# Two layers' first norm: the sums are turned before they are scaled, and 1/rms is put on eight units at eviction

## What is computed

```python
x = x + peer_ffn(h2, ...)                 # end of the first block
x = rmsnorm(x, g_final)                   # x / sqrt(mean(x*x) + 1e-6) * g_final
for l in range(2):                        # the two layers
    h = rms_norm(x, norm1_g[l])
    z = h @ w_in[l]                       # 9 projections of 512 and the 4096 gate columns
    za, zb, zc, zd, zg = split(z)         # retention, conv, gmlp, window attention, gates
    a, gate = split(zb)                   # conv branch
    u = a * sigmoid(gate)                 # then a 31-tap depthwise convolution, layer norm, silu
    x = x + (mix of the four branches) @ w_out[l]
    h = rms_norm(x, norm2_g[l])
    x = x + (silu(gt) * up) @ w_ffn_out[l]
```

## Time and profile before

| | us |
|---|---|
| median of 3 runs | 2181.37 (2179.74 to 2186.02) |
| the profiled execution's own time | 2182.02 |
| its span in the trace | 2180.3 |
| TensorE busy in the span | 2145.6 (98%) |
| VectorE, ScalarE, GpSimd busy | 1345.5, 1230.4, 970.7 |
| mean granted TensorE clock | 0.997 of full speed |
| DMA: bytes and mean rate | 370.16 MB, 170 GB/s |

### The profile page before, as it was taken

How to read it: one execution, slowest core, us unless ns; L and a number is a source line. 1 busy time by engine, 2 the same in 40 slices (tenths; PEclk the granted TensorE clock), 3 DMA queues, 4 the chain that set the end, 5 groups by cost and what they waited for, 6 DMA issues and landing times.

```text
span 2180.3 us, 38720 instructions
## 1 busy us (share of the span) xinstructions
PE 2145.6 (98%) x15148; PEld 2013.9 (92%) x15148; DVE 1345.5 (62%) x2626; ACT 1230.4 (56%) x2201; POOL 970.7 (45%) x791
## 2 busy tenths in 40 slices
PE   8999999999999999999999999999999999999999
PEld 7898989999999998888888899999998999899997
DVE  3547652998666766666665765356664854546664
ACT  5667554456777765555555556645445465655443
POOL 4675546999666650000004785560001876561000
PEclk9999999999999999999999999999999999999999
DMA  6544455656444456666665554455665545455665
GB/s 210 155 144 126 155 184 171 187 181 187 145 139 144 144 172 204 193 194 193 194 193 169 181 164 144 129 178 171 185 200 164 181 145 160 132 164 170 187 193 157
DMA packets 102952, 370.16 MB, mean 170 GB/s; under 512 B 11370, under 2 KB 12787, under 8 KB 102133
## 3 DMA queue, kind: packets, MB, share of 16 engines
q1 hardware_dynamic: 102772, 367.69, 54.4%
HBM read 365.53 MB, written 2.11 MB: 169 GB/s over the span
## 4 chain that ended last, share of the span: by engine, by line
PE 87%; DVE 6%; ACT 4%; issue 1%; POOL 1%; DMA 1%; SPq 0%; DVEq 0%; ACTq 0%; POOLq 0%
PE stream_bank L557 16%; PE stream_bank L559 16%; PE stream_bank L558 16%; PE side_bank L557 11%; PE side_bank L558 11%; PE side_bank L559 10%; PE side_bank L846 1%; PE side_bank L845 1%; ACT unit_hi L1114 1%; PE side_bank L635 1%; DVE swa_var L2277 1%; POOL unit_lo L2414 1%; PE side_bank L682 1%; DVE unit_lo L1658 1%; PE side_bank L662 1%
## 5 line engine op out<-in xcount | busy, mean ns | idle before, releaser
L2414 POOL TENSOR_TENSOR unit_lo<-raw,unit_hi 128x512 fp32r<-128x512 f32 (+1 forms) x724 | 932.3, 1314 | 403.3 <-ACT unit_hi L1114 401.8
L1114 ACT ACTIVATE unit_hi<-raw 128x1024 fp32r<-128x1024 f32 (+1 forms) x678 | 708.5, 1045 | 197.5 <-PE side_bank L559 74.6
L1658 DVE TENSOR_TENSOR unit_lo<-raw,unit_hi 128x1024 fp32r<-128x1024 f32 (+1 forms) x316 | 390.2, 1235 | 225.5 <-ACT unit_hi L1114 225.1
L557 PE MATMUL stream_bank<-hT_hi,unit_hi 128*128 128x256 f32 x1360 | 402.1, 296 | 3.1 <-POOL unit_lo L2414 3.1
L559 PE MATMUL stream_bank<-hT_hi,unit_lo 128*128 128x256 f32 x1360 | 387.3, 285 | 0.0
L558 PE MATMUL stream_bank<-hT_lo,unit_hi 128*128 128x256 f32 x1360 | 387.1, 285 | 0.0
L557 PE MATMUL stream_bank<-h2T_hi,unit_hi 128*128 128x256 f32 x1152 | 329.6, 286 | 0.0
L559 PE MATMUL stream_bank<-h2T_hi,unit_lo 128*128 128x256 f32 x1152 | 326.0, 283 | 0.0
L558 PE MATMUL stream_bank<-h2T_lo,unit_hi 128*128 128x256 f32 x1152 | 325.8, 283 | 0.0
L557 PEld LDWEIGHTS stream_bank<-hT_hi,unit_hi 128*128 128x128 f32 x1360 | 262.8, 193 | 10.5 <-issue 4.6
L558 PEld LDWEIGHTS stream_bank<-hT_lo,unit_hi 128*128 128x128 f32 x1360 | 263.0, 193 | 1.5
(11 more groups left out here) (355 smaller groups left out, 4526.3 us busy)
## 6 DMA issues: line engine op xcount, KB each, us to landing
raw<-in_peer_u_dram SPq DMA_DIRECT2D x128, 512.0 KB, 3.6
raw<-in_peer_v_dram SPq DMA_DIRECT2D x128, 512.0 KB, 3.6
raw<-in_gate_dram SPq DMA_DIRECT2D x64, 512.0 KB, 3.6
raw<-in_gt_dram SPq DMA_DIRECT2D x44, 512.0 KB, 4.2
raw<-in_up_dram SPq DMA_DIRECT2D x44, 512.0 KB, 4.2
raw<-in_ffn_out_dram SPq DMA_DIRECT2D x44, 512.0 KB, 4.2
raw<-in_branch_dram SPq DMA_DIRECT2D x32, 512.0 KB, 3.7
raw<-in_w_gate_dram SPq DMA_DIRECT2D x24, 512.0 KB, 3.6
```

Source lines behind the costliest of these rows:

```text
L557: mm(out, l.hi, r.hi, start=start, stop=False)
L1114: activation(k.unit_hi[n % SPLIT_SLOTS][:, 0:w], k.raw[n % RAW_SLOTS][:, 0:w], ACT.Copy).then_inc(k.sem("unit_hi"), 1)
L1658: V.tensor_tensor(k.unit_lo[s][:, 0:w], k.raw[n % RAW_SLOTS][:, 0:w], k.unit_hi[s][:, 0:w], ALU.subtract).then_inc(unit_lo, 1)
L2414: last = G.tensor_tensor(k.unit_lo[s][:, cols], k.raw[n % RAW_SLOTS][:, cols], k.unit_hi[s][:, cols], ALU.subtract)
```

## The change

- The sums of X are turned as they are, with the identity, as soon as VectorE has added them (`added_turns` with `norm_turns(..., scaled=False)`); the gain goes on when the turned rows are split. For layer 0 the gain is g_final times norm1. The pair goes to `turned_sums` (in `ys`), not to `hT2`. The three `keep_warm` are gone.
- cg and ca are multiplied from this unscaled pair, and VectorE puts 1/rms on each of the eight units: cg by one product out of the bank (ScalarE's tanh then follows in place), ca by one product within the bank ahead of L2310. 1/rms comes as rows, by `token_rows` (two matmuls with ones, behind cg.1) and a copy.
- The scaled pair for all the later units is built in rounds 1 to 6: in rounds 1 to 4 VectorE writes two chunks each of `scaled` out of the banks, in rounds 4 and 5 ScalarE writes the high parts, in rounds 5 and 6 VectorE the low parts (two 128x512 subtractions in each). rqk.0 waits for them.
- Layer 0: both norms are worked out at once. VectorE multiplies X by g_final (`x_gained`, four pieces), ScalarE sums the squares of both. The final norm's output is written to X piece by piece in rounds 2 to 5 (`final`), the fourth ahead of the low parts in round 5.
- SyncE loads three units more before the constants' fetch, which still waits for the fourth `x_final`. GpSimd's masking moves from the layer's start to the round of gv.3. The bias table moves from round 6 to round 11.

The diff, cut to its core:

```diff
@@ pe_program
-        keep_warm("nl")
 
     def layer(l):
-        keep_warm(name("n1"))
-        for _ in norm_turns(k.X, name("n1")):
+        sums = "peer_v" if l == 0 else f"ffn_out.{l - 1}"
+        for _ in added_turns(lambda h, t: (sums, t, h), name("n1")):
             pass
         def bias_tables():
-            for _ in range(5):
+            for _ in range(10):
...
             for i in range(KM):
-                fm_unit(name("cg"), i, k.hT2, KD, ready=chunks_of(name("n1")) if i == 0 else None)
+                fm_unit(name("cg"), i, k.turned_sums, KD,
+                        ready=(lambda c: (k.sem("turned_lo"), KD // 2 * l + c // 2 + 1)) if i == 0 else None)
+                if i == 1:
+                    token_rows(name("n1"))
+                yield
+            for i in range(KM):
+                fm_unit(name("ca"), i, k.turned_sums, KD)
+                yield
+            for i in range(8):
+                fm_unit(name("rqk"), i, k.hT2, KD,
+                        ready=(lambda c: (k.sem("scaled_lo"), KD // 2 * l + c // 2 + 1)) if i == 0 else None)
@@ act_program, layer
-        norm_stats(name("n1"), k.X, ready, k.squares4)
-        for _ in norm_hi(name("n1"), name("norm1"), k.hT2):
+        turned = norm_hi(name("n1"), "final" if l == 0 else name("norm1"), k.turned_sums)
+        activation(k.small("root_t", 1), k.ones[:, 0:1], ACT.Sqrt)
+        next(turned)
+        for t in range(TILES):
+            for h in range(2):
+                act.wait_ge(*k.over[sums, t, h])
+            last = activation(junk[:, t, :], k.X[:, t, :], ACT.Square, accum_out=sq[:, t:t + 1])
+            next(turned)
+        for _ in turned:
             pass
+        def statistics():
+            done = last
+            if l == 0:
+                for t in range(TILES):
+                    act.wait_ge(k.sem("x_gained"), 2 * t + 2)
+                    done = activation(k.xg[:, t, :], k.xg[:, t, :], ACT.Square,
+                                      accum_out=sq[:, TILES + t:TILES + t + 1])
+            done.then_inc(k.sem("norm_squares"), 1)
+            roots = r if l == 0 else r[:, 0:TILES]
+            act.wait_ge(k.sem("norm_sums"), STATS[name("n1")])
+            activation(roots, roots, ACT.Sqrt, scale=1.0 / D).then_inc(k.sem("norm_roots"), 1)
+            yield
+            yield
+            yield
+            for k2 in range(KD // 2):
+                act.wait_ge(*k.over[name("n1"), k2])
+                pair = slice(2 * k2, 2 * k2 + 2)
+                split_hi(k.hT2.hi[:, pair, :], k.scaled[:, pair, :], "scaled_hi")
+                if k2 == 1:
+                    yield
+            yield
@@ dve_program, layer
+        def gained(t, cols):
+            V.tensor_tensor(k.xg[:, t, cols], k.X[:, t, cols], k.g_final[:, cols], ALU.mult).then_inc(k.sem("x_gained"), 1)
...
+            for t, cols in pieces[0:2]:
+                gained(t, cols)
+        for _ in norm_lo(name("n1"), gain, k.turned_sums, (k.sem("turned_lo"), 1)):
+            pass
+        if l == 0:
+            for t, cols in pieces[2:4]:
+                gained(t, cols)
...
+        norm_diag(name("n1"), inverse[:, inverse.shape[1] - TILES:])
+        inverse = k.inverse_rms[:, :]
+        dve.wait_ge(k.sem("token_rows"), 2 * l + 1)
+        V.tensor_copy(inverse, k.bank[SIDE + 4][:, 0:TOKENS]).then_inc(k.free[SIDE + 4], 1)
+        def scaled_rows():
+            def low(k2):
+                pair = slice(2 * k2, 2 * k2 + 2)
+                dve.wait_ge(k.sem("scaled_hi"), KD // 2 * l + k2 + 1)
+                V.tensor_tensor(k.hT2.lo[:, pair, :], k.scaled[:, pair, :], k.hT2.hi[:, pair, :], ALU.subtract).then_inc(
+                    k.sem("scaled_lo"), 1)
+            for k2 in range(KD // 2):
+                for j in range(2):
+                    c = 2 * k2 + j
+                    last = V.scalar_tensor_tensor(k.scaled[:, c, :], k.bank[SIDE + k2][:, j * TOKENS:(j + 1) * TOKENS],
+                                                  k.gain(gain, c), inverse, ALU.mult, ALU.mult)
+                last.then_inc(k.free[SIDE + k2], 1)
+                if k2 and l == 0:
+                    final(*pieces[k2 - 1])
+                yield
+            if l == 0:
+                final(*pieces[3])
+            low(0)
+            low(1)
+            yield
+            low(2)
+            low(3)
+            yield
...
             for i in range(KM):
-                advance(name("cg"), i)
+                n = advance(name("cg"), i)
+                V.tensor_tensor(k.cv[:, i, :], k.bank[b][:, 0:TOKENS], inverse, ALU.mult).then_inc(k.free[b], 1)
...
+                own.then(V.tensor_tensor(product, product, inverse, ALU.mult))
+                V.scalar_tensor_tensor(cu, k.cv[:, i, :], 1.0, product, ALU.add,
...
-        at.run(main(), [bias_tables() if l == 0 else iter(()), own_channels(), sides()])
+        at.run(main(), [scaled_rows(), bias_tables() if l == 0 else iter(()), own_channels(), sides()])
@@ sp_program
-    load_until(U["cg.0", 0] + 6)
+    load_until(U["cg.0", 0] + 9)
     sp.wait_ge(k.sem("x_final"), 4)
     fetch(k.lc[:, :], a["layer_consts"], "landed_layer_consts")
```

More of the change, by code:

```diff
@@ L331, in col, with gain @@
         return self.cols[:, a + i:a + i + n]
+    def gain(self, name, c):
+        return self.small("final_gain", KD)[:, c:c + 1] if name == "final" else self.col(name, c)
     def small(self, name, n):
@@ L1688, in norm_lo @@
                 last = V.scalar_tensor_tensor(out.lo[:, c, :], k.bank[SIDE + k2][:, j * TOKENS:(j + 1) * TOKENS],
-                                              k.col(gcol, c), out.hi[:, c, :], ALU.mult, ALU.subtract)
-            last.then_inc(k.free[SIDE + k2], 1)
+                                              k.gain(gcol, c), out.hi[:, c, :], ALU.mult, ALU.subtract)
+            last.then_inc(*(done or (k.free[SIDE + k2], 1)))
             yield
@@ L2107, in layer @@
             advance(f"ffn_out.{l - 1}", KF - 1)
-        for _ in norm_lo(name("n1"), name("norm1"), k.hT2):
-            pass
-        V.memset(k.cu[:, :, 0:TAPS2 - 1], 0.0)
-        taps = k.col(name("conv_w2"), 0, TAPS2 * KM)
-        own.then(V.tensor_scalar(taps, taps, 0.5, None, ALU.mult))
-        if l == 0:
-            dve.wait_ge(k.sem("landed_layer_consts"), 16)
+        dve.wait_ge(k.sem("norm_squares"), STATS[name("n1")])
+        if l == 0:
+            own.then(V.tensor_scalar(r[:, 0:TILES], sq[:, 0:TILES], EPS * D, None, ALU.add))
+            last = V.scalar_tensor_tensor(r[:, TILES:], r[:, 0:TILES], EPS, sq[:, TILES:], ALU.mult, ALU.add)
+            inverse = r
+        else:
+            last = V.tensor_scalar(r[:, 0:TILES], sq[:, 0:TILES], EPS * D, None, ALU.add)
+            inverse = r[:, 0:TILES]
@@ new lines, in layer @@
+        last.then_inc(k.sem("norm_sums"), 1)
+        dve.wait_ge(k.sem("norm_roots"), STATS[name("n1")])
+        own.then(V.reciprocal(inverse, inverse))
+        norm_diag(name("n1"), inverse[:, inverse.shape[1] - TILES:])
+        inverse = k.inverse_rms[:, :]
+        dve.wait_ge(k.sem("token_rows"), 2 * l + 1)
+        V.tensor_copy(inverse, k.bank[SIDE + 4][:, 0:TOKENS]).then_inc(k.free[SIDE + 4], 1)
+        dve.wait_ge(*k.over[name("n1"), "rows"])
+        def scaled_rows():
[13 more added lines that the diff above has]
+                yield
+            if l == 0:
+                final(*pieces[3])
[5 more added lines that the diff above has]
+            yield
@@ L2116, in bias_tables, with final @@
+        def final(t, cols):
+            V.scalar_tensor_tensor(k.X[:, t, cols], k.X[:, t, cols], r[:, t:t + 1], k.g_final[:, cols], ALU.mult,
+                                   ALU.mult).then_inc(k.sem("x_final"), 1)
         def bias_tables():
-            for _ in range(5):
+            for _ in range(10):
                 yield
@@ L2483, in layer @@
         name = lambda s: f"{s}.{l}"
-        if l == 0:
-            pool.wait_ge(k.sem("landed_layer_consts"), 16)
-        pool.wait_ge(k.sem("landed_ws"), 16 * (l + 1))
-        for i in range(4):
-            cols = slice(i * P, (i + 1) * P)
-            last = G.tensor_tensor(k.ws[:, cols], k.ws[:, cols], k.tril, ALU.mult)
-        last.then_inc(k.sem("ws_masked"), 1)
         def gating_norm():
@@ L2494, in gating_norm @@
                 yield
+            pool.wait_ge(k.sem("landed_ws"), 16 * (l + 1))
+            for i in range(4):
+                cols = slice(i * P, (i + 1) * P)
+                last = G.tensor_tensor(k.ws[:, cols], k.ws[:, cols], k.tril, ALU.mult)
+            last.then_inc(k.sem("ws_masked"), 1)
             for t in range(TILES):
```

91 lines of the change are left out of this document (52 added, 39 removed).

## The result

The changed kernel is **slower: 2196.36 us median** (5 runs, 2195.01 to 2198.45); the ratio to the kernel before on the same chip is 1.0056, 95% interval 1.0044 to 1.0067, which is 9.6 to 14.6 us. The forecast was 2188.5 and its range ended at 2192: right sign, size too small. One term of the difference is the base: the median of three runs that I started from, 2181.37, was low; over 24 runs beside the first experiments the kernel before took 2184.14. Two executions of the kernel before that took far longer (7470 and 3299 us) are not compared.

What follows compares the result with a forecast made beforehand. TensorE's queue was taken to bound the kernel. Losses of 0.8 us in layer 0, 5.0 in layer 1 and 1.5 for the clock, 7.3 in all, on the median of 2181.37 gave 2188.5; range 2179 to 2192.

Steps and rivals of the forecast that it cites:

- Mechanism: Both layers: openings end ca.0 earlier, but VectorE's added work delays the third rotation; 7.3 us slower in all.
- The gain of the openings: Start of each layer: ca.0 ends 6.1 us earlier in layer 0, 0.9 us earlier in layer 1.
- Layer 1: ca.0 ends at 1689.2, VectorE frees the bank at 1716.2, so the third rotation comes 5.0 us late.
- the clock down behind it: Behind layer 1's third rotation: a wait over 3 us lowers TensorE's clock, 1.5 us added.
- The collisions of the low parts: Rounds 5 and 6, layer 1: VectorE's four low parts meet GpSimd's, 2.6 us added, bounds 0 and 5.2.
- Layer 0: Constants' fetch delays rqk.1, a 4.6 us wait plus 1.5 for the clock; third rotation at 1202.9, 0.8 us lost.
- now waits a little for VectorE's bias operation: Layer 0, second rotation: a small wait for VectorE's bias operation in the same bank, no size stated.
- both are about equally late: Layer 0, third rotation: TensorE's order gives about 1202.9, VectorE's own chain 1202.4.
- (a): Rival: stalls are there but smaller, without collisions (-2.6), fallen clock (-1.5) or both; 2184.6 to 2187.2, chance 0.30.
- (b): Rival: VectorE keeps up, bank free within 21 us of ca.0's end; 2174.4 (0.05), or 2180.5 with constants' wait left (0.08).
- (c): Rival: idle bits around cg.0 lower the clock at the openings too, 1.5 us each; 2190.2 to 2191.7, chance 0.15.
- (d): Rival: cg.0 cannot start early because banks, table load or additions hold the turning back; 2181 to 2184, chance 0.07.

Runs made afterwards that it cites:

- the first experiments: Follow-up runs measured against the kernel before on the same chip; over 24 runs beside them the kernel before took 2184.14 us.
- run 1: Changed kernel with VectorE's convolution taps spread otherwise, 16 instead of 31 in the first 8 steps: 2185.93 us, ratio 1.0009 to the kernel before.
- run 3: Changed kernel without most of the scaled pair's four low parts in layer 1, leaving out needed work: 2188.61 us, ratio 1.0021 to the kernel before.
- run 6: Kernel before with only the convolution taps spread otherwise: 2185.44 us, ratio 1.0007 to the kernel before.
- run 2: Changed kernel with rqk.1's load moved ahead of the constants' fetch in layer 0: 2197.18 us, ratio 1.0053 to the kernel before.
- run 5: Changed kernel with both the taps spread otherwise and rqk.1's load ahead of the constants' fetch: 2182.28 us, ratio 0.9988 to the kernel before.
- run 4: Kernel before with only the small preparations (8 gain columns, smaller table, product of the gains): 2183.4 us, ratio 1.0000 to the kernel before.

## Why the prediction was right or wrong

**Mechanism: right.** The gain of the openings is there and VectorE's queue takes it back at the rotations; runs 1, 3 and 6 show it, runs 2 and 5 that in layer 0 SyncE's constants' fetch stands in series with it.

**Layer 1: right.** ca.0 ends at about 1695.7, 1689.6 on the time scale of before (predicted 1689.2). The third rotation comes at 1716.6 (predicted bank free at 1716.2), 5.4 us late (5.0), with the clock down behind it (1.5). The collisions of the low parts, the middle of a range of 0 to 5.2, were 4.93 - 2.5 = 2.4 us (2.6). The stretch is 7.1 us longer; 5.0 + 1.5 were forecast. I had read the Trainium skill ("SBUF — State Buffer", section Terms) as if each of the four would wait for a whole instruction of GpSimd, 2.6 us more. What it says is that the port pair is held for a full instruction and the loser blocks until then, which can be less than a whole one; these rows, with half of that time, agree with this and not with my reading.

**Layer 0: the step that failed.** The forecast was 0.8 us lost, the trace shows 4.3 at the third rotation. The places on the time scale of before: cg.0's turning as foreseen; the token rows at 1166.1 instead of 1164.9, since beside GpSimd VectorE's last two products with g_final took 2.39 us (I had 1.2) and the taps' scaling 1.18 (0.16 in the trace of before), and a unit's low part, 1.23 us, stood ahead of the diagonals too. So ca.0 ends at 1175.2 instead of 1174.1, and the constants' fetch is issued at 1178.0 instead of 1176.5:

```profile
1175.01 0.33 SPq L2657 DMA_DIRECT2D raw<-in_rqk_dram  x1
1179.79 0.33 SPq L2667 DMA_DIRECT2D layer_consts<-in_layer_consts_dram  x1
```

rqk.1 starts at 1191.0 instead of 1190.2, 0.8 us. The other 2.8 come at the next place, the second rotation, which "now waits a little for VectorE's bias operation". In the sum that gave 1202.9 this "little" is 0.9 us (what is left beside the units, the rotations, the bias product and one low clock), and it has no fall of the clock behind it. The wait was 1.86 us, 1.0 more, and the clock fell once more, 1.5 us: from this rotation to the third are 4.90 us and from there to the fourth (1211.57) 3.30.

VectorE's queue, which sets this wait, was summed too short:

```profile
1193.01 2.16 DVE L1705 TENSOR_TENSOR unit_lo<-raw,unit_hi 128x1024 fp32r<-128x1024 f32 x1
...
1202.77 0.55 DVE L2222 TENSOR_TENSOR bias_rows<-side_bank,bias_consts 8x384 f32<-8x384 f32 x1
...
1205.79 0.42 DVE L2305 TENSOR_TENSOR ret_qk<-ret_qk,side_bank 128x256 f32<-128x256 f32 x1
```

The first rotation's bank was free at 1205.79 + 0.42 - 1.8 = 1204.4, where I had 1202.4. Of these 2.0 us 1.1 are ca.0's later end and 0.9 the low part of VectorE's own unit, 2.16 us instead of 1.22, a collision for which the prediction had nothing. And I took "both are about equally late" for harmless, though the place where they meet is a wait with a clock behind it.

**The base: 2.8 us.** 2184.1 and not 2181.4 is the level of before. The execution that I read, 2182.02, lay 2.1 us below it, and its layer 0 was 2 us shorter than those of runs 4 and 6, so most of this is likely one and the same thing. With the measured layers, 4.3 + 7.1 = 11.4, or some 9.4 against the layer 0 of run 4, 2184.1 gives 2193.5 to 2195.5 for the 2196.4 measured. The 11.4 lies within the interval of 9.6 to 14.6, the 9.4 just below it; what remains has no place that these traces show. So of the 7.9 us between the forecast and the measured time 2.8 are the base, 3.5 the step in layer 0, 0.6 layer 1, and 1.0 is left.

**The rivals.** (a) fell: collisions and clock were both paid. (b) fell for this kernel, but run 5 shows its point of decision: with some 5.8 us of taps (the estimate of run 1) taken from ahead of the bank and the load moved, the time ends below before, as (b) had it, though by 2 us and not 7. (c) fell: behind the openings the clock stays at 1.00, even after the 2.29 us before the token rows. I had its price in the range's end, for another place: a further fall came, but at the rotation. The Trainium skill, "TensorE: Matmul & The Clock Gate", Part 1, tells of a kernel whose TensorE idled briefly so often that its clock swung between the two levels; at these openings the trace doesn't show that. (d) fell: cg.0 starts 7.8 us earlier.

## What to carry to other kernels

Work moved off the critical path goes into some engine's queue; find the next instruction in that queue that the bound engine waits for, and count the slack there, for every such place and not for the last one only. Where two queues deliver in series, an edit of one can show nothing and still be half of the cure: try them together. And take the level of before from many runs before an effect of 0.5% is forecast to the microsecond.

## What I had not expected of the hardware

In these traces the clock doesn't follow the length of a single wait: after 2.29 us (ahead of the token rows) and after 1.90 us (layer 1's third rotation in run 3) it stayed at 1.00, after 1.86 us (second rotation of layer 0) and after 2.1 us (before cg.3 in run 4) it fell to 0.50. Once down, it stayed there for 3 to 7 us: in run 1 the windows from 1193 to 1200 are near 0.50, in the changed kernel those from 1194 to 1198. A 256-wide matmul then starts every 0.21 us instead of 0.12, so a fall costs 1.5 to 3 us, an estimate from these spacings. The prediction took it that 1.92 us of waiting lowers the clock and 1.51 doesn't; these waits give no such limit.

An untouched stretch of code can differ between executions by a step: from the first peer_v load to the last it is 350.2 us in four of the fourteen traces and 351.8 to 351.9 in ten, with nothing between. Not every stretch does so: from the first peer_q load to the first peer_u load the values spread from 50.3 to 52.4.
